# Expert results stored by token and choice; all but the last three blocks read back early, the last three summed by products

## The chip, the cores and the metric

One core of a Trainium2 chip runs the whole kernel. The metric is the device time of one execution in microseconds. TensorE is PE in the profile, its weight loads PEld, VectorE DVE, ScalarE ACT, GpSimd POOL and SyncE SP.

## The reference

Two transformer blocks on 512 tokens of width 1024, all in float32. The first block and the second's mixer are not touched. The change lies in the last layer, a mixture of experts with 32 experts of which each token takes two, and in the last normalisation:

```python
def hierarchical_moe(h, rg_w, rg_b, re_w, re_b, w_gate, w_up, w_down):
    ...
    gate = p_grp * jax.nn.softmax(top_val, axis=-1)
    expert_id = grp[:, None] * EXPERTS_PER_GROUP + top_idx.astype(jnp.int32)
    ...
    def expert_block(args):
        xb, e = args
        a = xb @ w_gate[e]
        u = xb @ w_up[e]
        return (jax.nn.silu(a) * u) @ w_down[e]

    ys = lax.map(expert_block, (xs, block_expert)).reshape(n_slots, D)
    ys = ys * slot_gate[:, None].astype(ys.dtype)
    out = jnp.zeros((T, D), ys.dtype).at[slot_tok].add(ys)
    return out.reshape(B, S, D).astype(h.dtype)

...
        h = rmsnorm(x, norm_ffn_g[l])
        x = x + hierarchical_moe(h, router_group_w[l], router_group_b[l],
                                 router_expert_w[l], router_expert_b[l],
                                 expert_w_gate[l], expert_w_up[l], expert_w_down[l])
    return rmsnorm(x, final_norm_g)
```

`top_val` holds the two best of a token's expert scores, `slot_tok` and `slot_gate` the token and the gate of each place in the padded blocks. w_gate and w_up are 1024x512, w_down is 512x1024: 2 MB each, 6 MB for an expert.

## The kernel before

The program is written by hand, one instruction stream for each engine; semaphores set the order. `Queue.step` lets an instruction raise its engine's semaphore, `run` also waits for it, `wait` waits for other engines' steps.

Dense stages come first (lines 196 to about 1500). At their start GpSimd makes the masks (lines 202 to 214) for which the other engines wait, then index tables (221 to 228). In the first feed-forward stage ScalarE clears the buffer of expert results in HBM, `y_d`, with one transfer of 8 MB (line 427).

Router (1585 to 1720): VectorE finds two experts for each token and a place for each of the 1024 pairs of token and choice. Pairs are cut into blocks of BS = 32 rows of one expert, and the blocks stand in turns of SETS = 3. Products with one-hot tables (1734) give for each block and row the token, a large number where the row is padding. GpSimd gathers a block's rows from `h_d` (1761) by that table. An index beyond the bound is skipped. SyncE loads weights (954), only when the expert of that set of buffers changes; three sets are in use, so the loads for a block are issued when the block three places earlier has finished with the buffer. The loads of the down weights of two sets wait for the first gather (1580).

The block loop (1838 to 2003) runs per block: `gate_up` (1850, the products of 32 rows with both matrices, four groups of 32 columns of the array side by side), transposes of the next block's rows (1768), `down` of the block before (1868), and four products that turn the gated halves (1876). ScalarE copies the first products (1882), applies SiLU (1887), and copies half of the down result (1892); VectorE keeps the turned rows (1809), copies one column of indices (1773), adds the halves of the result into `y_e` (1909) and multiplies (1920). ScalarE then stores `y_e`, 32 rows in two halves of 512 columns, into `y_d` by block position (1902), padding too. GpSimd's part of the loop is the gather for a later block (1950, 1761). The number of turns is computed on the chip.

After the last store GpSimd waits and issues eight indirect loads of 128 rows of 4 KB (2014), one for each tile of 128 tokens and each choice. VectorE multiplies them by the gates and adds them to the tokens (2026), ScalarE squares and sums, VectorE scales by the root (2029 to 2041), and SyncE stores the output (2043).

## Time and profile before

| | us |
|---|---|
| median of 3 runs | 2011.5 (2010.38 to 2014.53) |
| profiled execution | 2010.09 |
| its span | 2008.8 |
| TensorE busy | 1814.8 (90%), granted clock 0.952 |
| VectorE / ScalarE / GpSimd busy | 846.3 / 437.2 / 982.7 |
| HBM read / written | 475.06 MB / 19.66 MB |

The dense stages take the first 1457 us, the router runs to about 1482, the blocks to 1977 and the end of the kernel to 2008.8. Times in all views count from the start of the span. Busy shares are means over stages with different limits, so the stages are read one by one.

### The profile page before, as it was taken

How to read it: one execution, taken by the hardware profiler on the slowest of the kernel's cores; microseconds unless marked ns; L12 is line 12 of the kernel's file. 1: busy time of each engine (PE TensorE's matmuls, PEld its weight loads, DVE VectorE, ACT ScalarE, POOL GpSimd, SP SyncE). 2: the span in 40 equal slices, each digit the busy share in tenths (PEclk: the TensorE clock that was granted, in tenths of full speed). 3: DMA queues.
4: the chain of work that ended last, by engine and by line, in shares of the span. 5: the costliest groups of instructions: out<-in, count | busy, mean ns of one | idle time of the engine just before them, and what ended most of it. 6: DMA issues, size and time to landing. Idle time of an engine off the chain costs nothing.

```text
span 2008.8 us, 27496 instructions
## 1 busy us (share of the span) xinstructions
PE 1814.8 (90%) x9716; PEld 1274.7 (63%) x9716; DVE 846.3 (42%) x1248; ACT 437.2 (22%) x813; POOL 982.7 (49%) x532
## 2 busy tenths in 40 slices
PE   8999999999999899999999889998968978969783
PEld 6888888887676678888888656765733333323231
DVE  6444433310444577444444489876341111111114
ACT  3111100100344432111100144552421111111112
POOL 6888887777444378888887533321211111101001
PEclk9999999999999999999999989999979989979887
DMA  4333372433111133333333212210588999999995
GB/s 160 94 96 102 106 267 88 145 94 94 53 57 50 43 89 91 101 95 94 94 112 100 73 53 73 66 54 28 235 312 325 401 403 399 401 415 412 411 393 207
DMA packets 56977, 346.00 MB, mean 172 GB/s; under 512 B 8474, under 2 KB 8858, under 8 KB 44896
## 3 DMA queue, kind: packets, MB, share of 16 engines
q1 hardware_dynamic: 44640, 315.12, 43.0%
q10 hardware_dynamic: 7968, 19.46, 2.6%
q0 software_dynamic: 4320, 10.78, 1.6%
q8 instruction: 29, 0.48, 0.1%
q14 instruction: 20, 0.16, 0.0%
HBM read 475.06 MB, written 19.66 MB: 246 GB/s over the span
## 4 chain that ended last, share of the span: by engine, by line
PE 71%; DMA 14%; DVE 10%; ACT 3%; issue 1%; POOL 1%; SPq 0%; DVEq 0%; ACTq 0%; POOLq 0%
PE bank L471 31%; PE bank L442 12%; DMA big<-w_up_in 11%; PE bank L1850 7%; PE bank L723 4%; PE bank L1349 4%; PE bank L1868 2%; DVE big L1075 2%; PE bank L490 2%; PE bank L1463 2%; DMA ring<-w_down_in 1%; PE bank L1876 1%; PE bank L641 1%; DVE state L1060 1%; PE bank L701 1%
## 5 line engine op out<-in xcount | busy, mean ns | idle before, releaser
L282 POOL TENSOR_TENSOR weights_hi_parts<-ring,ones 128x1024 fp32r<-128x1024 f32 (+1 forms) x174 | 351.4, 2019 | 291.9 <-PE bank L471 127.7
L284 POOL TENSOR_TENSOR ring_parts<-ring,weights_hi_parts 128x1024 fp32r<-128x1024 f32 (+1 forms) x174 | 468.7, 2693 | 13.6
L471 PE MATMUL bank<-attention_buffers_parts,weights_hi_parts 128*128 128x512 f32 x832 | 325.6, 391 | 11.4 <-DVE ring_parts L510 10.0
L471 PE MATMUL bank<-state_parts,weights_hi_parts 128*128 128x512 f32 x832 | 324.4, 390 | 0.0
L471 PE MATMUL bank<-attention_buffers_parts,ring_parts 128*128 128x512 f32 x832 | 324.2, 390 | 0.0
L1850 PE MATMUL bank<-big,work 128*32 128x512 f32 x1440 | 227.5, 674 | 51.3 <-DMA big<-w_up_in 51.1
L442 PE MATMUL bank<-big_parts,weights_hi_parts 128*128 128x512 f32 x704 | 216.8, 389 | 1.2 <-POOL ring_parts L284 1.2
L1950 POOL TENSOR_TENSOR small<-small 128x1 f32<-128x1 f32 x51 | 9.6, 189 | 375.0 <-DVE small L1773 375.0
L895 POOL TENSOR_TENSOR ring_parts<-ring,weights_hi_parts 128x1024 fp32r<-128x1024 f32 x32 | 80.6, 2520 | 222.6 <-ACT weights_hi_parts L892 222.6
L471 PEld LDWEIGHTS bank<-attention_buffers_parts,weights_hi_parts 128*128 128x128 f32 x832 | 156.6, 188 | 44.8 <-issue 10.5
L471 PEld LDWEIGHTS bank<-state_parts,weights_hi_parts 128*128 128x128 f32 x832 | 156.6, 188 | 33.0 <-issue 0.5
L471 PEld LDWEIGHTS bank<-attention_buffers_parts,ring_parts 128*128 128x128 f32 x832 | 156.6, 188 | 32.8
L442 PEld LDWEIGHTS bank<-big_parts,weights_hi_parts 128*128 128x128 f32 x704 | 132.0, 188 | 29.2 <-POOL ring_parts L284 2.0
L1809 DVE TENSOR_TENSOR work<-bank,cols 128x256 f32<-128x256 f32 x54 | 22.9, 424 | 296.3 <-PE bank L1768 296.3
L1850 PEld LDWEIGHTS bank<-big,work 128*32 128x32 f32 x1440 | 58.1, 122 | 133.0 <-issue 131.5
L442 PE MATMUL bank<-big_parts,ring_parts 128*128 128x512 f32 x352 | 137.0, 389 | 0.0
L413 DVE TENSOR_TENSOR work<-bank,token_scale 128x512 f32<-128x512 f32 x44 | 30.4, 691 | 194.7 <-PE bank L471 194.7
L320 DVE TENSOR_TENSOR big_parts<-work,big_parts 128x512 f32 (+1 forms) x44 | 82.9, 1884 | 42.3 <-ACT big_parts L318 42.3
L1882 ACT ACTIVATE weights_hi<-bank 128x512 f32<-128x512 f32 x54 | 32.3, 597 | 302.7 <-PE bank L1850 302.7
L1850 PE MATMUL bank<-attention_buffers,work 128*32 128x512 f32 x288 | 75.6, 672 | 21.7 <-DMA big<-w_up_in 21.2
L1075 DVE SCALAR_TENSOR_TENSOR big<-big,cols 128x512 f32<-128x512 f32 x105 | 91.5, 919 | 5.9 <-ACT big L1069 5.3
L318 ACT ACTIVATE big_parts<-work 128x512 f32 (+1 forms) x44 | 27.9, 633 | 280.8 <-DVE work L415 280.8
(391 smaller groups left out, 2833.6 us busy)
## 6 DMA issues: line engine op xcount, KB each, us to landing
big<-w_up_in SPq DMA_DIRECT2D x54, 2048.0 KB
ring<-wdense_in SPq DMA_DIRECT2D x176, 512.0 KB, 3.5
state<-w_down_in SPq DMA_DIRECT2D x37, 2048.0 KB
big<-w_gate_in SPq DMA_DIRECT2D x36, 2048.0 KB
attention_buffers<-w_gate_in SPq DMA_DIRECT2D x18, 2048.0 KB
ring<-w_down_in SPq DMA_DIRECT2D x18, 2048.0 KB
ring<-wff_in SPq DMA_DIRECT2D x32, 704.0 KB, 4.1
y_rows<-big ACTq DMA_DIRECT2D x1, 8192.0 KB, 28.0
```

Of the source, the lines that this page charges most:

```text
L282: po.tensor_tensor(hi, raw, ones[:, 0:1].to_broadcast([128, words]), ALU.mult).then_inc(PO.sem, 1)
L284: po.tensor_tensor(lo, raw, hi.bitcast(F32), ALU.subtract) \
L320: return DV.step(dv.tensor_tensor(lo, raw, hi.bitcast(F32), ALU.subtract))
L442: m = pe.matmul(bank, x, y_, start=t + k + n == 0, stop=t == 1 and k == h - 1 and n == 2)
L471: m = pe.matmul(out, x, y_, start=j + n == 0, stop=j == len(pairs) - 1 and n == len(ts) - 1)
L490: m = pe.matmul(banks[t][:, :], x, y_, start=k + n == 0, stop=k == KD - 1 and n == len(ts) - 1)
L723: m = pe.matmul(banks[7][:, :], x, y_, start=k + t == 0, stop=k == KD - 1 and t == 2, skip_group_check=True)
L895: lo_made[n] = PO.step(po.tensor_tensor(lo, raw, hi.bitcast(F32), ALU.subtract))
L1075: last = DV.step(dv.scalar_tensor_tensor(dst, src, w, dst, ALU.mult, ALU.add))
L1349: m = pe.matmul(banks[bank][:, :], x, y_, start=k + j == 0, stop=k == KD - 1 and j == 2, skip_group_check=True)
L1463: m = pe.matmul(bank[:, :], x, y_, start=k == 4 and n == 0, stop=k == 3 and n == 2, skip_group_check=True)
L1850: m = pe.matmul(first_products[b][p:p + BS, :], xet[:, (k + odd) * BS:(k + odd + 1) * BS], sets[b][m_][:, (k + odd) * D_EXP:(k + odd + 1) ...
```

## The change

The buffer of results is now indexed by choice, token and half row: 2048 half rows of 512 numbers and a few spare ones. An indirect DMA by GpSimd scatters each block's 64 half rows (`scatter_step`), in which the indices of padding lie beyond the bound. The half rows of the first partition of each half always have an index within it, if need be that of a spare row. The gates are no longer applied at the end: ScalarE's copy of the first products scales the rows of the up product by their gate (`row_scale`), for which products with the one-hot tables spread the gates over rows (64 more TensorE instructions behind the first `gate_up`). SyncE reads the first choices (`s_pick`) and GpSimd adds the second choices into the tokens by accumulating DMAs (`s_second`) when all turns but the last are scattered. The last three blocks are not stored; one-hot tables made on VectorE (`one_hot`) and products on TensorE (`to_tokens`) sum them by token in PSUM. VectorE adds the first choices (`add_first`) and the banks. The one-hot tables of the router have moved to other buffers; two scale tables became one allocation. GpSimd makes four constant columns at the start with ten more small instructions, VectorE makes three tables of 64x67 in the router (`row_tok`, `row_at`, `added_to`) with four. Tiles 2 and 3 of `to_tokens` follow tile 1 with three calls each. In the diff, cut:

```diff
@@ start @@
-    zeros = big[:, 44 * T:44 * T + D]
+    zeros = big[:, 44 * T:44 * T + 512]
     cleared = PO.run(po.memset(zeros, 0.0))
+    for b in range(SETS):
+        po.dma_start(y_d[4 * T + 2 * b:4 * T + 2 * b + 2, :], zeros[0:2, :]).then_inc(s_y[b], 16)
...
@@ clearing @@
-            ac.dma_start(y_d.rearrange("(n p) c -> p n c", p=128),
-                         zeros.unsqueeze(1).to_broadcast([128, Y_ROWS // 128, D])).then_inc(s_fill, 16)
+            ac.dma_start(y_d[0:4 * T, :].rearrange("(n p) c -> p n c", p=128),
+                         zeros.unsqueeze(1).to_broadcast([128, 4 * NT, 512])).then_inc(s_fill, 16)
@@ router @@
+    DV.step(dv.tensor_scalar(all_but_two.bitcast(I32), turn, -2.0, None, ALU.add))
...
+    def by_rows(bank, cols_, table, copies):
+        for c in range(C2):
+            for g in range(copies):
+                m = pe.matmul(bank[g * BS:(g + 1) * BS, cols_], oh_row[:, c * BS:(c + 1) * BS],
+                              table[:, c * SLOT_COLS:(c + 1) * SLOT_COLS], start=c == 0, stop=c == C2 - 1,
+                              tile_position=(0, g * BS))
+        return m
+    s = PE.step(by_rows(banks[2], slice(0, SLOT_COLS), oh_tok, 2))
...
+    DV.run(dv.tensor_scalar(tokens[:, SETS:], tokens[:, SETS:], NO_ROW + T - 1, None, ALU.bitwise_and))
...
-    DV.run(dv.scalar_tensor_tensor(posf, place, float(BS), rmod, ALU.mult, ALU.add))
-    DV.run(dv.tensor_copy(pos.bitcast(I32), posf))
...
+    gated_slots = DV.run(dv.tensor_tensor(by_slot(oh_gate), by_slot(oh_slot), over_last(gates, C2, SLOT_COLS), ALU.mult))
...
+    dv.wait_ge(s_spread, 1)
+    dv.tensor_scalar(row_scale, banks[7][:, 0:SLOT_COLS], is_up, not_up, ALU.mult, ALU.add).then_inc(DV.sem, 3)
@@ block loop @@
-        ac.activation(gu, first_products[c % SETS][:, :], ACT.Copy).then_inc(AC.sem, 1)
+        ac.activation(gu, first_products[c % SETS][:, :], ACT.Copy,
+                      scale=row_scale[:, bass.ds(i * SETS + c, 1)]).then_inc(AC.sem, 1)
...
-            ac.dma_start(y_d[bass.ds(i * (SETS * BS) + c * BS, BS), half * 512:half * 512 + 512],
-                         y_e[c % SETS][half * BS:(half + 1) * BS, :]).then_inc(s_y[c % SETS], 16)
...
     def dve_result(i, c, steps=1):
+        dv.wait_ge(s_y[c % SETS], i * 16 + (16 * (c // SETS) + 16))
+        dv.tensor_copy(to[c % SETS].bitcast(I32), added_to[:, bass.ds(i * SETS + c, 1)].bitcast(I32)).then_inc(DV.sem, 1)
         dv.wait_ge(AC.sem, at_step(AC, AC_Y, i, c + 1))
-        dv.wait_ge(s_y[c % SETS], i * 32 + (32 * (c // SETS) + 16))
...
+    by_token = y_d[0:4 * T, :].rearrange("(r h) c -> r (h c)", h=2)
+    sp.wait_ge(PE.sem, at_step(PE, PE_GU, laps["sp"], 0))
+    for b in range(SETS):
+        sp.wait_ge(s_y[b], laps["sp"] * 16 + 16)
+    for t in range(NT):
+        sp.dma_start(att[:, t * D:(t + 1) * D], by_token[t * 128:(t + 1) * 128, :]).then_inc(s_pick[t], 16)
...
+    def scatter_step(i, c, n):
+        po.wait_ge(PO.sem, i * (2 * SETS) + (pool_begun + n))
+        po.wait_ge(DV.sem, at_step(DV, DV_Y, i, c + 1))
+        po.tensor_tensor(zo, zc, zc, ALU.add).then_inc(PO.sem, 1)
+        po.indirect_dma_start(y_d[:, :], bass.IndirectOffsetOnAxis(ap=to[c].bitcast(U32), axis=0), y_e[c], None,
+                              bounds_check=4 * T + 1, oob_is_err=False).then_inc(s_y[c], 16)
...
+        for c in range(SETS):
+            gather_step(i, c + 2, 2 * c + 2)
+            scatter_step(i, c, 2 * c + 3)
...
+    for b in range(SETS):
+        po.wait_ge(s_y[b], before_last * 16 + 32)
+    po.wait_ge(s_wexp[2][2], before_last * 16 + 48)
...
+    for t in range(NT):
+        po.dma_start(x_tok[:, t * D:(t + 1) * D], by_token[T + t * 128:T + (t + 1) * 128, :],
+                     accum_op=ALU.add).then_inc(s_second[t], 16)
@@ end, VectorE @@
+    def add_first(t):
+        xt = x_tok[:, t * D:(t + 1) * D]
+        dv.wait_ge(s_pick[t], 16)
+        dv.wait_ge(s_second[t], 16)
+        return DE.run(dv.tensor_tensor(xt, xt, first_rows_at[:, t * D:(t + 1) * D], ALU.add))
...
     dve_mul(laps["dv"], 2)
+    add_first(0)
+    dv.wait_ge(s_y[2], laps["dv"] * 16 + 16)
     dv.wait_ge(AC.sem, at_step(AC, AC_SILU, laps["dv"], 2) + 1)
+    last_sum = DE.step(dv.tensor_tensor(y_e[2], results[2][0:2 * BS, :], y_odd, ALU.add))
+    add_first(1)
@@ end, TensorE @@
+    def to_tokens(t, c):
+        for half in range(2):
+            p = half * BS
+            m = pe.matmul(banks[2 * t + half][:, :], to_token[c][p:p + BS, t * 128:(t + 1) * 128], y_e[c][p:p + BS, :],
+                          start=c == 0, stop=c == SETS - 1, tile_position=(p, 0))
+        return m
+    pe.wait_ge(DV.sem, at_step(DV, DV_Y, laps["pe"], 1))
+    to_tokens(0, 0)
     down(laps["pe"], 2)
+    pe.wait_ge(DV.sem, at_step(DV, DV_Y, laps["pe"], 2))
+    to_tokens(0, 1)
+    to_tokens(1, 0)
+    PE.wait(last_sum)
+    summed = [PT.step(to_tokens(0, 2))]
+    to_tokens(1, 1)
+    summed.append(PT.step(to_tokens(1, 2)))
...
-            for j in range(2):
-                s = DE.run(dv.scalar_tensor_tensor(xt, picked[t][j], gates[:, j * NT + t:j * NT + t + 1], xt, ALU.mult, ALU.add))
+            if t > 1:
+                add_first(t)
+            DE.wait(summed[t])
+            for half in range(2):
+                xh = x_half(t, half)
+                s = DE.step(dv.tensor_tensor(xh, banks[2 * t + half][:, :], xh, ALU.add))
```

## Rows read from the trace of the kernel before

**Rows 1.** Windows: busy us of each engine, granted clock, DMA share, GB/s

```profile
1472.00:1482.00 10.00, 5.61 (x32) 5.23 (x32) 6.61 (x25) 0.00 (x0) 2.17 (x3) 0.50 0.12 42
1486.00:1528.00 42.00, 34.21 (x284) 13.59 (x280) 5.57 (x17) 5.88 (x12) 5.51 (x10) 0.91 1.01 397
1530.00:1560.00 30.00, 30.00 (x275) 12.32 (x278) 6.55 (x18) 6.25 (x14) 4.42 (x8) 1.00 0.76 275
1560.00:1948.00 388.00, 319.32 (x2640) 127.06 (x2636) 57.84 (x164) 60.24 (x123) 45.30 (x82) 0.90 1.01 408
1964.00:1970.00 6.00, 6.00 (x60) 2.66 (x62) 1.35 (x4) 1.39 (x3) 0.00 (x0) 1.00 0.68 265
1970.00:1978.00 8.00, 5.60 (x52) 1.94 (x43) 1.60 (x3) 2.06 (x4) 0.00 (x0) 1.00 0.07 16
```

**Rows 2.** Chain of waits from 1923 us to the end: start, us, what

```profile
1923.66 19.55 DMA big<-w_up_in
...
1972.64 1.05 PE bank L1876 x8
...
1974.44 1.96 PE bank L1868 x16
...
1977.05 0.69 DVE ring L1985
...
1980.44 0.53 issue
1980.97 0.98 POOL big L2014
...
1982.25 5.69 DMA big<-y_rows,small
1987.96 1.29 DVE big L2026
...
1993.24 0.17 DVE small L2029
...
1995.22 1.21 DVE big L2026
...
2004.87 1.28 DVE big L2041
```

**Rows 3.** DMA issues: KB of each, median us from issue to landing

```profile
y_rows<-ring ACTq DMA_DIRECT2D x108, 64.0 KB, 6.8
...
h_rows<-state POOLq DMA_DIRECT2D x4, 512.0 KB, 10.8
out<-big SPq DMA_DIRECT2D x4, 512.0 KB, 2.6
```

**Rows 4.** Queues of the page (packets, MB, share) and its HBM line

```profile
q0 software_dynamic: 4320, 10.78, 1.6%
...
HBM read 475.06 MB, written 19.66 MB: 246 GB/s over the span
```

**Rows 5.** Windows of line 1909 alone, VectorE's sum of a block's result

```profile
1560.00:1943.00 383.00, 27.99 (x41) 0.90 1.01 408
```

**Rows 6.** Timeline of the router's end: start, us, instruction

```profile
1475.80 1.99 PE L471 MATMUL bank<-work 128*32 128x67 f32 x16 [7.47 <-DVE work L1732]
...
1482.31 0.81 SPq L952 DMA_DIRECT2D state<-w_down_in  x2
```

**Rows 7.** Chain of waits in two earlier stretches, 0 to 60 and 1440 to 1700

```profile
22.82 0.86 PE bank L374 x2
...
1497.79 28.12 DMA ring<-w_down_in
```

**Rows 8.** A group of the page: an addition out of PSUM

```profile
L413 DVE TENSOR_TENSOR work<-bank,token_scale 128x512 f32<-128x512 f32 x44 | 30.4, 691 | 194.7 <-PE bank L471 194.7
```

**Rows 9.** Timeline of the program's start

```profile
3.53 0.29 POOL L213 TENSOR_SCALAR_AFFINE_SELECT tri_strict<-ones 128x128 f32<-128x128 f32 x1
...
6.28 1.33 ACT L366 ACTIVATE attention_buffers_parts<-state,cols 128x512 fp32r<-128x512 f32 x2 [3.54 <-DMA cols<-cols_in]
```

More of the change, by code:

```diff
@@ L1663, in build @@
     heads, ids1, key, ahead = sm(3), sm(C2), sm(33), sm(1)
-    pair, total, most, rest, turn = sm(1), sm(1), sm(1), sm(1), sm(1)
+    pair, total, most, rest, all_but_two, turn = sm(1), sm(1), sm(1), sm(1), sm(1), sm(1)
     shift, past, unfilled = sm(2), sm(1), sm(1)
@@ L1700, in build @@
     rank, rdiv, rmod = sm(C2), sm(C2), sm(C2)
-    place, late, posf, pos = sm(C2), sm(C2), sm(C2), sm(C2)
+    place, late, later = sm(C2), sm(C2), sm(C2)
     picks_jn = picks.rearrange("p (j n) -> p j n", j=2)
@@ L1717, in build @@
     DV.step(dv.tensor_scalar(late, place, turn, shift[:, 0:1], ALU.is_ge, ALU.mult))
-    DV.run(dv.tensor_scalar(posf, place, past, shift[:, 1:2], ALU.is_ge, ALU.mult))
-    DV.run(dv.tensor_tensor(late, late, posf, ALU.add))
+    DV.run(dv.tensor_scalar(later, place, past, shift[:, 1:2], ALU.is_ge, ALU.mult))
+    DV.run(dv.tensor_tensor(late, late, later, ALU.add))
     DV.run(dv.tensor_tensor(place, place, late, ALU.add))
-    oh_row, oh_slot = work[:, 512:512 + C2 * BS], work[:, 1536:1536 + C2 * SLOT_COLS]
-    oh_tok, oh_exp = work[:, 2072:2072 + C2 * SLOT_COLS], hi_raw[:, 2 * D:2 * D + C2 * SLOT_COLS]
-    assert 512 + C2 * BS <= 1536 and C2 * SLOT_COLS <= 536 and 2 * D + C2 * SLOT_COLS <= 2 * SLOT
+    n_oh = C2 * SLOT_COLS
+    oh_slot, oh_tok, oh_exp = ring[:, 0:n_oh], ring[:, n_oh:2 * n_oh], hi_raw[:, 2 * D:2 * D + n_oh]
+    oh_gate, oh_row = both_scales[:, 0:n_oh], both_scales[:, n_oh:n_oh + C2 * BS]
+    assert 2 * n_oh <= SETS * 512 and n_oh + C2 * BS <= 2 * T and 2 * D + n_oh <= 2 * SLOT
     def by_slot(x):
@@ L1755, in build @@
     gu, hg, het = hi_raw[:, 2048:2560], hi_raw[:, 2560:2560 + 4 * BS], hi_raw[:, 2688:2688 + 4 * BS]
-    idx = [sm(1) for _ in range(SETS)]
+    idx, to = [sm(1) for _ in range(SETS)], [sm(1)[0:2 * BS, :] for _ in range(SETS)]
     laps = {}
@@ L1778, in build @@
         gather(b, tokens[:, b:b + 1])
-    for q in (PE, AC, PO, DV):
+    PO.wait(counted_laps)
+    laps["po"] = po.value_load(all_but_two[0:1, 0:1].bitcast(I32), min_val=lo - 1, max_val=hi - 1)
+    for q in (PE, AC, DV):
         q.wait(counted_laps)
@@ L1827, in build @@
     AC_GU, AC_Y, AC_SILU = range(1, 4)
-    DV_X, DV_IDX, DV_Y, DV_MUL = range(1, 5)
+    DV_X, DV_IDX, DV_TO, DV_Y, DV_MUL = range(1, 6)
     def at_step(q, k, i, c):
```

117 lines of the change are left out of this document (70 added, 47 removed).

## The prediction

> **What bounds the kernel now.** I read the share of the DMA engines first, then the chain of waits, then the queues, because the diff touches one stage and the end of the program. Up to about 1480 us the kernel is dense matrix work that the diff leaves alone but for a few instructions at the very start. The expert stage behind it is bound by its transfers: from 1560 to 1948 us the 16 DMA engines are busy at a share of 1.01 and move 408 GB/s [rows 1]. TensorE is busy for 319 of these 388 us; the chain of waits shows loads of the up-projection that take 20 us from issue to landing, far longer than 2 MB need at 408 GB/s (5.1 us), since they stand behind other loads [rows 2]. So in this stretch the time is bytes divided by bandwidth. From 1530 to 1560 us the share is 0.76 [rows 1]: there TensorE sets the pace, and bytes saved are worth nothing. From 1943 us on the chain is TensorE again, four more blocks, and then a tail without products: the last sum ends at 1977.74, its rows are stored, GpSimd begins to issue indirect loads at 1980.97, one of them takes 5.69 us to land, VectorE starts at 1987.96 and ends at 2006.15 [rows 2]. These 28.4 us are what the change rebuilds.
>
> **1. Fewer bytes in the saturated stretch.** Before, each of the 54 blocks stores all of its 32 rows of 4 KB in two transfers of 64 KB [rows 3]. The reference has 512 tokens with two experts each, so 1024 of 54 x 32 = 1728 rows are real and 704 (40.7%) are padding. The new store is an indirect one that skips padding. That the chip really moves nothing for a skipped row shows in the software queue: stores of 512 rows of h, 1024 rows read back at the end and 54 gathers of 32 rows of 4 KB would be 13.4 MB if all rows moved; the queue's row has 10.78 MB, which is 1024 real rows in the gathers and few more [rows 4]. In the stretch from 1560 to 1943 us 41 blocks write their results [rows 5]: 41 x 131 KB = 5.37 MB, of which 40.7% = 2.19 MB go away. At 408 GB/s that is 5.4 us. Bounds: 0, if the busiest DMA engine gets no less work, and 7.6 us, if all 54 blocks and a little more counted (54 x 131 KB x 0.407 / 408 = 7.1, and the gathers land sooner). I take -5.4, because the share of 1.01 over the whole stretch leaves no idle time in which the saving could vanish.
>
> The Trainium skill, page "DMA: Bandwidth & Descriptors", section "The descriptor swizzle", speaks against this: it gives each engine four neighbouring partitions. By that rule the filled rows of a block, which lie in its lowest partitions, would keep the same engines as busy as before, and the sum would lose its 5.4 us. No row here names the engine of a packet. It is the second rival below.
>
> **2. What the new store costs its engines.** ScalarE loses two issues per block. GpSimd gains a step per block: a small addition, 0.53 of issue and an indirect DMA of 0.98 us [rows 2], 1.7 us in all. 41 of them add 70 us to the 45.3 that GpSimd is busy in 388 us [rows 1], so it stays two thirds idle. The gather is ahead of the scatter in its queue as on VectorE, so no gather waits behind a scatter whose data come later. VectorE gains one copy of one column; its next sum into the same buffer waits for a scatter from three blocks earlier, and such transfers land in about 7 us [rows 3]. Taken as 0. If the cover were gone, a gather late by 2 us would hold TensorE for as much in each block that TensorE paces.
>
> **3. The front of the stage.** The DMA engines are nearly idle from 1472 to 1482 us (share 0.12 [rows 1]) and the load that ends this starts at 1482.31, behind the first gather [rows 6]. So everything ahead of that gather moves the whole stage. Added there: one VectorE step of some 0.1 us, and a second copy of the products that place the tokens. One copy takes 1.99 us for 16 instructions [rows 6]; the second goes to other columns of the array, as the four groups of L1868 do, where 8 products in 16 instructions take 1.96 us [rows 2] though one alone takes 0.86 [rows 7]. So +0.2, with bounds 0 and +2.1. Behind the gather come five small VectorE operations (0.2 us each), one of 0.7 for the gate table, 64 TensorE instructions for the gates (2 us side by side, 8 one after another) and a wait of the first block's ScalarE copy for them. From 1486 to 1528 us the DMA engines are full (1.01 [rows 1]) and the chain ends in a load of 28.12 us [rows 7], issued into a queue with two earlier pairs of loads in it. These 2 to 8 us lie beside it: 0. Without that cover they would cost 2.5.
>
> **4. The start of the program.** Three small transfers are issued by GpSimd ahead of the masks for which the engines wait. Masks end at 3.82, ScalarE starts at 6.28, when its columns are in [rows 9]. Half the clearing is gone (-0.5), three issues of 0.5 us with gaps of 0.3 and 0.5 ahead of them come in: masks at about 6.1. Cost 0 to 1, taken as +0.2. The table of results that is cleared shrinks by half in a stage with idle DMA: 0.
>
> **5. The tail.** Second choices are added into the token rows by an accumulating DMA from GpSimd and first choices are read by SyncE, four transfers of 512 KB each, when the scatters before the last three blocks have landed; the last three blocks reach the tokens through one-hot products. The one-hot tables (12 small VectorE operations) fall into waits of VectorE. From the rows of the chain and of an addition out of PSUM [rows 2, 7, 8], with 0.86 us for a pair of products (two halves, side by side in different rows of the array):
> TensorE is free at 1973.69; the first pair holds it to 1974.55, so the last down products start 0.11 late and end at 1976.51; copy 0.65 with its gaps, sum 0.69: last sum at 1977.85. Meanwhile two pairs (to 1978.23) and the pair that needs the sum: 1979.1. VectorE adds first choices of tile 1 (1.29) and then two halves out of PSUM at 0.69 each: 1980.6. Tile 1's two pairs end at 1980.8, its halves at 1982.2. Scaling of tile 0 (0.17 + 0.2 + 0.2 + 1.28 with gaps: 1.98): 1984.2. Tiles 2 and 3 cost 1.29 + 1.4 + 1.98 each: 1988.9 and 1993.6; the last scaling ends at 1995.5. Before: 2006.15. That is -10.6.
> The risk is in order: on VectorE the addition of tile 0, which waits for both transfers, stands ahead of the last sum. GpSimd waits for the last down weights, which land near 1969 (the share is 0.68 from 1964 to 1970 us and 0.07 behind it [rows 1]); 0.7 us later it issues. 512 KB land in 2.6 us when stored alone and in 10.8 among other traffic [rows 3]. The trace has no accumulating DMA. Bounded from below by the 512 KB store and from above by that 10.8 for a first tile, it lands between 1973 and 1981, the next ones 1.3 to 9 us apart; it is needed at 1975.7 to cost nothing. Nearest is a shared, otherwise idle queue with twice the traffic (it reads and writes the rows): tile 0 at about 1976.5, a cost of 1.0. I take -9.6 for the tail, bounds -10.6 and -3.
>
> Sum: -5.4 + 0.2 + 0.2 - 9.6 = -14.6. The profiled execution took 2010.09 us (span 2008.8), so 1995.5; the median of the runs shown, 2011.5, lies 1.4 above it. Forecast **1996.9 us**.
>
> **Rivals.** (a) Pairs of products don't run side by side, or TensorE's clock falls from 2.4 to 1.2 GHz in the tail, so that a pair takes 1.72. The same walk gives: last sum 1978.7, tile 0 summed at 1984.0, tile 3's products at 1996.3, end 2001.6; the tail saves 4.5 and the time is 2002.0. For it: the trace shows groups of columns side by side, never of rows. Against: the clock is 1.00 up to 1978 although TensorE has gaps there [rows 1], and the tail now has fewer. The Trainium skill, "TensorEngine Tiling (Array Packing)", section "Tiling Modes", has row tiles work in parallel; that favours the forecast.
> (b) The skipped rows relieve only engines that weren't the last ones, so the stretch keeps its length: 2002.3. For it: a load ends with its slowest engine. Against: the gathers, which have the same skipped rows, leave the share at 1.01 as a mean over all 16.
> (c) Slower than before: the accumulating DMA is slow. All the rest saves about 5 us elsewhere, so the change loses from the point at which the fourth tile lands after 2005 (6.6 us of VectorE's work stand behind it, and 2006.15 + 5 is the mark), that is 2.1 MB in 35 us, 60 GB/s or a seventh of the stretch's rate. At 50 GB/s it lands at 2013 and the end is 2019.6, 13.5 later than now; less the 5 saved elsewhere the time is 2020. For it: no row prices it, and it stands ahead of the last sum. Against: an indirect load of 512 KB on the same queue lands in 5.69 us [rows 2].
> (d) The change doesn't do what it says: readback isn't early, because SyncE and GpSimd wait for the scatters of the last but one lap; if these land 7 us late under load, tile 0 is there at 1981 and the tail saves 5: 2001.5.
>
> **Numbers.** Forecast 0.50; (a) 0.14; (b) 0.18; (d) 0.06; (c) 0.07; two of a, b and d together (about 2007) 0.05. Below: both bounds good, 1991. The range 1991.5 to 2005 leaves out (c), most of the pairs and little below. A measurement of this kernel tells 0.2%, 4 us, from no change. Faster 0.87, same 0.05, slower 0.08.
>
> **What would show it.** Right: written HBM bytes down from 19.7 to about 12.6 MB (4.2 less for the clearing, 2.9 less padding); the last gate and up load landing 5 us earlier; about 19 us from the last sum to the end in place of 28.4; one-hot pairs of 0.9 us. Wrong: a share of 1.0 and the last load at 1943 as before (b); pairs of 1.7 us (a); VectorE waiting for the accumulated rows ahead of the last sum (c, d); a first gather more than 1 us later.

## The result, and the profile after

The changed kernel took 2005.62 us (median of 7 runs, 2004.23 to 2010.76) beside 2012.81 for the kernel before on the same chip (7 runs): ratio 0.9968, 95% interval 0.9956 to 0.998. It is faster by 6.4 us, 4.0 to 8.9; the forecast had 14.6. The profiled execution took 2005.99 us, span 2004.4, against 2010.09 and 2008.8: 4.1 us less. The two numbers differ because the profiled run of before lay under its median.

The queues of the page (packets, MB, share) and its HBM line, after:

```profile
q0 software_dynamic: 6288, 12.81, 2.1%
...
HBM read 475.06 MB, written 15.09 MB: 245 GB/s over the span
```

Three windows of [rows 1] for after, the window of [rows 5] for all engines, and four of the tail: busy us of PE, PEld, DVE, ACT, POOL, granted clock, DMA share, GB/s:

```profile
1486.00:1528.00 42.00, 36.02 (x358) 14.90 (x351) 6.14 (x22) 6.41 (x13) 8.91 (x17) 0.92 1.01 395
1530.00:1560.00 30.00, 30.00 (x276) 12.08 (x272) 6.01 (x20) 6.24 (x12) 9.88 (x17) 1.00 0.81 289
1560.00:1943.00 383.00, 310.65 (x2612) 124.58 (x2608) 61.63 (x205) 63.89 (x123) 91.71 (x164) 0.90 1.00 404
1560.00:1948.00 388.00, 315.65 (x2644) 126.36 (x2638) 61.63 (x205) 64.31 (x124) 91.71 (x164) 0.90 1.00 402
...
1974.00:1976.00 2.00, 2.00 (x12) 0.68 (x8) 0.00 (x0) 1.62 (x2) 0.00 (x0) 1.00 1.07 268
1976.00:1978.00 2.00, 0.21 (x2) 0.00 (x0) 0.00 (x0) 0.46 (x2) 0.00 (x0) 0.81 1.06 223
1978.00:1982.00 4.00, 1.17 (x4) 0.66 (x6) 2.69 (x3) 0.00 (x0) 0.00 (x0) 0.50 1.06 211
1982.00:1986.00 4.00, 4.00 (x12) 1.52 (x10) 1.73 (x3) 1.15 (x2) 0.00 (x0) 0.50 0.78 155
```

The chain of waits that answers to [rows 2]:

```profile
1921.80 20.16 DMA big<-w_up_in
...
1957.28 11.26 DMA state<-w_down_in
...
1969.16 9.49 DMA big<-results_by_token
...
1978.74 1.24 DVE big L2048
...
1980.09 0.69 DVE ring L2066
...
1980.83 15.75 PE bank L2092 x36
...
2000.44 1.28 DVE big L2137
```

DMA issues (KB of each, median us to landing), answering to [rows 3]:

```profile
attention_buffers<-results_by_token SPq DMA_DIRECT2D x4, 512.0 KB, 6.6
big<-results_by_token POOLq DMA_DIRECT2D x4, 512.0 KB, 12.3
results_by_token<-ring,small POOLq DMA_INDIRECT x51, 6.8
```

Timeline lines of the program's start, of the router's end and of the tail:

```profile
6.46 1.33 ACT L381 ACTIVATE attention_buffers_parts<-state,cols 128x512 fp32r<-128x512 f32 x2 [3.74 <-POOL iota_f L230]
...
1476.30 2.00 PE L1757 MATMUL bank<-ring,_squares_and_token_scale 128*32 128x67 f32 x32 [7.51 <-DVE ring L1751]
...
1974.22 1.99 PE L2092 MATMUL bank<-ring,work 32*128 32x512 f32 x8
...
1978.74 1.22 DVE L2048 TENSOR_TENSOR big<-big,attention_buffers 128x1024 f32<-128x1024 f32 x1 [6.73 <-DMA big<-results_by_token]
...
1980.83 2.07 PE L2092 MATMUL bank<-ring,work 32*128 32x512 f32 x4 [4.62 <-DVE ring L2066]
```

Two places hold the difference. The last w_up load lands at 1941.95 instead of 1943.21: the stretch gave 1.3 us, 1.7 counted from the first block's first product (1484.38, before 1483.93). In the window to 1943 us the DMA engines are almost as full as before (share 1.00, before 1.01), but move 404 GB/s instead of 408 [rows 5]. (The 402 of the window to 1948 us has in it 6 us behind the last load, which came 1.3 us earlier than before.) From that landing to the last end it takes 59.8 us instead of 62.9, where the forecast had 53.3. In the chain VectorE waits 6.73 us for accumulated rows, adds them, and only then makes the last sum, which ends at 1980.78. TensorE stands idle for 4.62 us ahead of it; its granted clock falls from 1.00 to 0.81 and 0.50 (2.4 to 1.2 GHz), and its last 36 instructions, 9 pairs of products, take 15.75 us.

### The profile page after: what moved, and what is told of

It reads as the page before. It is cut to its first block, busy times and chain, and to the rows that moved or that the text cites. A ratio compares the mean times of both kernels' runs of the same rounds, so it can differ in the third digit from the quotient of the medians.

```text
span 2004.4 us, 27790 instructions
## 1 busy us (share of the span) xinstructions
PE 1830.3 (91%) x9844; PEld 1282.7 (64%) x9844; DVE 852.8 (43%) x1321; ACT 441.9 (22%) x813; POOL 1043.6 (52%) x643
## 3 DMA queue, kind: packets, MB, share of 16 engines
q0 software_dynamic: 6288, 12.81, 2.1%
HBM read 475.06 MB, written 15.09 MB: 245 GB/s over the span
## 4 chain that ended last, share of the span: by engine, by line
PE 71%; DMA 14%; DVE 10%; ACT 3%; issue 1%; POOL 1%; SPq 0%; DVEq 0%; ACTq 0%; POOLq 0%
PE bank L486 31%; DMA big<-w_up_in 13%; PE bank L457 12%; PE bank L1882 7%; PE bank L740 4%; PE bank L1366 4%; DVE big L1092 2%; PE bank L505 2%; PE bank L1900 2%; PE bank L1480 2%; PE bank L1908 1%; PE bank L658 1%; DVE state L1077 1%; PE bank L718 1%; PE bank L2092 1%
## 5 line engine op out<-in xcount | busy, mean ns | idle before, releaser
L428 DVE TENSOR_TENSOR work<-bank,_squares_and_token_scale 128x512 f32<-128x512 f32 x44 | 30.4, 690 | 194.7 <-PE bank L486 194.7
L1914 ACT ACTIVATE weights_hi<-bank,small 128x512 f32<-128x512 f32 x54 | 37.1, 687 | 309.2 <-PE bank L1882 283.6
L1882 PE MATMUL bank<-attention_buffers,work 128*32 128x512 f32 x288 | 72.1, 645 | 19.0 <-DMA big<-w_up_in 18.4
```

The costliest lines, as they stand in the source:

```text
L1882: m = pe.matmul(first_products[b][p:p + BS, :], xet[:, (k + odd) * BS:(k + odd + 1) * BS], sets[b][m_][:, (k + odd) * D_EXP:(k + odd + 1) ...
```

## The experiments

All are compared with the kernel before on the same chip, and a difference between two of them is that of their ratios times 2012 us. "Length" is the time from the first block's first product to the landing of the last w_up load in the profiled run. It is used because the dense part ahead of it varies: that first product lay anywhere between 1480.8 and 1489.0 us. A length is one profiled run. The changed kernel, e1 and e2 differ only behind the stretch and have 457.6, 457.3 and 456.5; e3, e6 and e8 have 451.9, 452.6 and 453.3. So a difference in length of about 1 us is within what runs differ by, and a difference of two ratios is uncertain by some 3 to 5 us (from their intervals).

| kernel | median us | ratio, 95% interval | length us |
|---|---|---|---|
| before | 2011 to 2013 | 1 | 459.3 |
| changed | 2005.62 | 0.9968, 0.9956 to 0.998 | 457.6 |
| e1_sum_first | 2003.13 | 0.9963, 0.9945 to 0.998 | 457.3 |
| e2_no_accumulate | 2004.36 | 0.9957, 0.9943 to 0.9971 | 456.5 |
| e3_rows_spread | 1999.35 | 0.9948, 0.9932 to 0.9964 | 451.9 |
| e4_padding_stored | 2006.83 | 0.9984, 0.9973 to 0.9994 | 459.3 |
| e5_half_stores | 2004.08 | 0.9963, 0.9952 to 0.9973 | 451.8 |
| e6_plain_reads | 1993.01 | 0.9916, 0.9899 to 0.9933 | 452.6 |
| e7_before_spread | 2006.69 | 0.9976, 0.9965 to 0.9987 | 452.7 |
| e8_reads_behind | 1996.31 | 0.9918, 0.9901 to 0.9934 | 453.3 |
| e9_all_gathered | 2015.87 | 1.002, 1.001 to 1.003 | 467.4 |
| e10_gathered_spread | 2014.59 | 1.0007, 0.9997 to 1.0016 | 467.7 |
| e11_before_gathered | 2021.82 | 1.0034, 1.0022 to 1.0047 | 471.0 |
| e12_upper_rows_skipped | 2006.78 | 0.9976, 0.9966 to 0.9986 | 457.4 |
| e13_odd_rows_skipped | 2001.46 | 0.9943, 0.9929 to 0.9957 | 452.7 |
| e14_spread_all_stored | 2004.25 | 0.9963, 0.9949 to 0.9977 | 454.7 |

### The tail: order, clock, accumulation

e1_sum_first changes the order on VectorE:

```diff
-    add_first(0)
     dv.wait_ge(s_y[2], laps["dv"] * 16 + 16)
     dv.wait_ge(AC.sem, at_step(AC, AC_SILU, laps["dv"], 2) + 1)
     last_sum = DE.step(dv.tensor_tensor(y_e[2], results[2][0:2 * BS, :], y_odd, ALU.add))
+    add_first(0)
     add_first(1)
```

> The changed kernel with the last block's sum ahead of the additions of tile 0's rows on VectorE, nothing else. Theory: the wait for the accumulated rows of tile 0 (landing at 1978.65) held the last sum by 5.1 us and left TensorE idle for 4.6 us, whereupon its clock fell to 1.2 GHz. Now the last sum ends 5 us earlier, the clock stays at 2.4 GHz, a pair of one-hot products takes 0.9 us in place of 1.75, and the end comes 3 to 4 us earlier: ratio to before 0.995. Rival (row tiles run one after another at any clock): pairs take 1.75 us still, end at most 1 us earlier.

Windows of e1, and its chain:

```profile
1974.00:1978.00 4.00, 4.00 (x28) 1.45 (x22) 0.68 (x1) 2.08 (x3) 0.00 (x0) 1.00 1.05 250
1978.00:1982.00 4.00, 4.00 (x22) 1.85 (x20) 1.23 (x1) 0.00 (x0) 0.00 (x0) 1.00 1.06 209
```

```profile
1970.66 11.41 DMA big<-results_by_token
...
1982.20 1.24 DVE big L2048
```

The last sum starts at 1976.10, TensorE doesn't stop, the clock stays at 1.00, and the products run on at 0.88 us a pair (11 pairs, 44 instructions, in 9.71 us). So pairs do run side by side; what made them 1.75 in the changed kernel is the clock, which fell because TensorE stood still. From the last w_up landing to the end it takes 55.3 us, 4.5 less than in the changed kernel. The rest of the gain doesn't come: VectorE now waits for the accumulated rows behind the last sum. Tile 0's let it start at 1979.69, 9.7 us after GpSimd's first issue at 1970.00; tile 1's land 11.41 us after the start given in the chain, and only then do the sums out of PSUM begin:

```profile
1979.69 1.23 DVE L2048 TENSOR_TENSOR big<-big,attention_buffers 128x1024 f32<-128x1024 f32 x1 [2.92 <-DMA big<-results_by_token]
1982.20 1.23 DVE L2048 TENSOR_TENSOR big<-big,attention_buffers 128x1024 f32<-128x1024 f32 x1 [1.28 <-DMA big<-results_by_token]
```

By the ratios e1 and the changed kernel can't be told apart (0.9963 and 0.9968); the gain is in the profile only.

e2_no_accumulate reads the second choices without adding, so that they are left out of the result:

```diff
-        po.dma_start(x_tok[:, t * D:(t + 1) * D], by_token[T + t * 128:T + (t + 1) * 128, :],
-                     accum_op=ALU.add).then_inc(s_second[t], 16)
+        po.dma_start(second_at[:, t * D:(t + 1) * D], by_token[T + t * 128:T + (t + 1) * 128, :]).then_inc(s_second[t], 16)
```

> The changed kernel, with its four late reads of second choices taken without adding, into a free buffer: the second choices of all but the last three blocks are left out of the result. Nothing else moves: GpSimd issues them at the same place, after the last w_down load. Theory (adding in memory makes these transfers move at half rate, and VectorE's first add stands ahead of the last sum): in the profile of the changed kernel the first of them landed 9.49 us after its issue (1978.65), at 211 to 223 GB/s with the DMA engines full; read plainly it should land 4 to 5 us after the issue, about 1974, so that the last sum comes at about 1976 instead of 1980.09, TensorE keeps its clock at 2.4 GHz over the 18 products behind it (about 8 us instead of 15.75), and the time falls by 4 to 8 us, to 1998 to 2002. Rival (the reads are only late because they share the queues with SyncE's reads of the first choices, 2 MB more): landing at 1978 as before, and 2005 to 2006.

A row of its chain, a window, and the last products:

```profile
1969.67 8.40 DMA big<-results_by_token
```

```profile
1974.00:1978.00 4.00, 4.00 (x28) 1.10 (x24) 0.16 (x1) 1.48 (x2) 0.00 (x0) 1.00 0.99 387
```

```profile
1980.26 15.73 PE L2092 MATMUL bank<-ring,work 32*128 32x512 f32 x36 [1.91 <-DVE ring L2066]
```

The chain decides for the rival, for the most part: a plain read lands 8.40 us after its issue, an accumulating one 9.49. The rate does differ: e2 moves 387 GB/s here, where the changed kernel has 268 and 223 in the two halves of this window. But tile 0 has to wait for SyncE's 2 MB beside it in either case. Adding in memory cost 1 to 2 us of the 5 that the sum was late (it ends 37.1 us after the last w_up landing, in the changed kernel 38.8, in e1 33.5); the place of the wait cost the rest. And a shorter wait did not bring the clock back: TensorE is idle for only 1.91 us here, yet the granted clock is at 0.68 from 1978 to 1982 us and at 0.50 behind it, and the 36 instructions take 15.73 us as before. The tail is 58.1 us, 1.7 less than in the changed kernel.

e6_plain_reads takes away both. On top of the spread rows (e3, below), SyncE reads both choices at once; GpSimd adds tiles 2 and 3:

```diff
     for t in range(NT):
         sp.dma_start(att[:, t * D:(t + 1) * D], by_token[t * 128:(t + 1) * 128, :]).then_inc(s_pick[t], 16)
+        sp.dma_start(second_at[:, t * D:(t + 1) * D], by_token[T + t * 128:T + (t + 1) * 128, :]).then_inc(s_second[t], 16)
...
-    po.wait_ge(s_wexp[2][2], before_last * 16 + 48)
...
+    for t in (2, 3):
+        xt = x_tok[:, t * D:(t + 1) * D]
+        po.wait_ge(s_pick[t], 16)
+        PA.run(po.tensor_tensor(xt, xt, att[:, t * D:(t + 1) * D], ALU.add))
+        po.wait_ge(s_second[t], 16)
+        pool_added[t] = PA.run(po.tensor_tensor(xt, xt, second_at[:, t * D:(t + 1) * D], ALU.add))
```

> The changed kernel with the rows of a block spread as in e3_rows_spread (1999.35 us), and in place of the four accumulating reads four plain ones by SyncE, each behind the first-choice read of its tile, without waiting for the last w_down load; GpSimd adds both choices of tiles 2 and 3, VectorE those of tiles 0 and 1. Theory (adding in memory costs twice the engine time, and holds VectorE ahead of the last sum): both choices of tile 0 are there at about 1964 to 1966, the last sum comes at about 1968 instead of 1972.25, the clock stays at 2.4 GHz, and the time is 1989 to 1993. Rival (2 MB more ahead of the last w_down load push that load back by their own 5 us): the last sum comes at 1972 to 1974 as before, the products still run at 2.4 GHz since TensorE waits for a load and not for VectorE in the same way, and the time is 1994 to 1998; 1999 if the clock falls too.

Timeline of its tail:

```profile
1965.24 9.71 PE L2098 MATMUL bank<-ring,work 32*128 32x512 f32 x44
...
1966.00 0.68 DVE L2072 TENSOR_TENSOR ring<-bank,work 64x512 f32<-64x512 f32 x1 [0.58 <-ACT work L2027]
...
1983.80 1.28 DVE L2143 SCALAR_TENSOR_TENSOR big<-big,small,weights_hi 128x1024 f32<-128x1024 f32 x1
```

The last sum waits for ScalarE's copy and for nothing else. It ends 33.2 us after the last w_up landing (38.8 in the changed kernel) and 18.4 us ahead of the end (20.9), at full clock: a tail of 51.6 us against 59.8. Against e3 that is worth 6.4 us. It has the lowest ratio here, 0.84% under the kernel before.

e8_reads_behind puts the second reads behind the last w_down load and the first adds behind the last sum, and moves the three clearing DMAs of the program's start behind the masks:

> e6_plain_reads with three things moved: the four plain reads of second choices wait for the last w_down load, VectorE's first adds stand behind the last sum, and GpSimd's three small clearing DMAs at the program's start stand behind its masks. Theory (a load that TensorE waits for must have nothing beside it; the last sum must not wait for a read): last sum some 2 us after the last w_down product, about 1967, clock 2.4 GHz, both choices of tile 0 at about 1968 to 1970, time 1987 to 1991; ScalarE's first operation at 6.28 again instead of 6.46, and all of the program 0.4 us earlier. Rival (VectorE is what is late: its eight adds of 1.24 us and eight sums of 0.69 us now stand behind one another after the last sum): 1992 to 1996, not under e6_plain_reads.

The rival holds: the sum starts at 1974.84, 33.0 us after the landing (32.6 in e6), but then four adds of VectorE lie behind it, 8.1 us up to the first sum out of PSUM, where e6 has two in 4.5 us, and the tail is 55.5 us. Reading early didn't hold the last sum back. By the ratios e8 and e6 can't be told apart. At the start, ScalarE begins at 6.29 without the three DMAs in front and at 6.23 in e6, which has them. The 0.18 us of the changed kernel's row are within what runs differ by.

### The stretch: bytes, and where they lie

e4_padding_stored gives padding rows spare rows of their own, so that nothing is skipped; e5_half_stores takes half the rows off the direct stores of the kernel before:

```diff
-            ac.dma_start(y_d[bass.ds(i * (SETS * BS) + c * BS, BS), half * 512:half * 512 + 512],
-                         y_e[c % SETS][half * BS:(half + 1) * BS, :]).then_inc(s_y[c % SETS], 16)
+            ac.dma_start(y_d[bass.ds(i * (SETS * BS) + c * BS, BS // 2), half * 512:half * 512 + 512],
+                         y_e[c % SETS][half * BS:half * BS + BS // 2, :]).then_inc(s_y[c % SETS], 16)
```

> The changed kernel, but padding rows are scattered too, each to a spare row of its own, so that every scatter moves all 64 half rows. Theory A (engines of the low partitions set the pace and are as busy either way): the last up-projection load lands within 1 us of the changed kernel's 1941.95, ratio to before about 0.997. Theory B (the skipped bytes save 5.4 us but the scatter costs as much by its packets): the landing is 5 to 6 us later, at about 1947, ratio 0.9995.

> The kernel before, but of each block only the first 16 of 32 rows are stored; the other rows' results are left out. The bytes go down by half on all DMA engines alike: 41 x 65.5 KB = 2.69 MB in the stretch, at 408 GB/s 6.6 us. Theory A (bytes count when every engine is relieved): the last up-projection load lands at 1936 to 1938 in place of 1943.21, ratio 0.9965. Theory C (bytes of stores don't matter in the stretch, since loads and stores go by different paths or another limit holds): landing within 1.5 us of 1943.2, ratio 0.999 to 1.0.

The software queue holds 15.38 MB in e4 and 12.81 in the changed kernel: padding is skipped, 2.57 MB of it. At 408 GB/s that would be 6.3 us. It is worth 1.7 in length and 3.2 in the ratios. ScalarE's queue is 3.53 MB smaller in e5 (19.46 and 15.93), 3.34 MB of it ahead of the last three blocks; that is worth 7.5 and 7.4 us, close to the 8.2 of 3.34 MB. So bytes off the stores can pay nearly in full, and the padding's don't. Full scatters in place of direct stores cost nothing that shows: e4 has the length of the kernel before.

e3_rows_spread deals the ranks of a block over its 32 rows, so that padding no longer lies in the last ones:

```diff
+    row_order = both_scales[:, 2 * T - BS:2 * T]
+    DV.step(dv.tensor_copy(row_order.rearrange("p (s o b) -> p b o s", o=2, b=2),
+                           iota_f[:, 0:BS].rearrange("p (b o s) -> p b o s", b=2, o=2)))
...
-    DV.step(dv.tensor_tensor(by_slot(oh_row), iota_f[:, 0:BS].unsqueeze(1).to_broadcast([128, C2, BS]),
+    DV.step(dv.tensor_tensor(by_slot(oh_row), row_order.unsqueeze(1).to_broadcast([128, C2, BS]),
```

> The changed kernel with one thing different: row j of a block no longer stands in partition j but the rows are dealt out so that any eight neighbouring partitions groups of four get every eighth row (a permuted table of 32 numbers in the router). Theory A (skipped rows relieve only some DMA engines, since filled rows stand together in the low partitions): the filled rows now load all engines alike, so the stretch from 1560 to 1943 us gets shorter; the last up-projection load lands at 1937 to 1939 in place of 1941.95, and the time is 3 to 5 us below the changed kernel's 2005.6, ratio to before about 0.995. Theory B (the scatter costs as much as the skipped bytes save, by its packets): no change, landing at 1941 to 1943, ratio 0.997.

The last w_up load lands at 1933.98, the length falls by 5.6 us and the time by 4.0 against the changed kernel, with the same bytes in every queue. But spreading could ease the gathers as well as the stores. e7_before_spread is the control, the same spreading in the kernel before (with the positions to read back taken from the spread rows):

> The kernel before, with the rows of a block spread over its 32 partitions as in e3_rows_spread and the positions to read back changed to match; every row is still stored. It separates the two things that the spreading may have eased in e3 (8 us at the last w_up load against the changed kernel): the stores, whose skipped rows exist only in the changed kernel, and the gathers of token rows, whose padding is skipped in both kernels. Theory (each DMA engine serves its own partitions, and padding that lies in the last rows leaves the engines of the first rows as they were): the gathers carry 4.49 MB where 51 full ones would be 6.68, so they may give at most 2.19 MB / 408 GB/s = 5.4 us, and at least the 8 - 6.2 = 1.8 us that skipped stores cannot explain: last w_up load 2 to 5 us ahead of 1943.21, time 2006 to 2010, less some 0.5 for two more small VectorE operations at the start of the blocks. Rival (only the stores gained): no change, 2011 to 2012.

It gains 4.8 us (6.6 in length) with no store skipped. So what e3 gained can all have been the gathers', which the change had left as they were. I then tried to take the gathers out of the question by filling them:

```diff
-    DV.run(dv.tensor_scalar(tokens[:, SETS:], tokens[:, SETS:], NO_ROW + T - 1, None, ALU.bitwise_and))
-    DV.run(dv.tensor_scalar(tokens[0:1, SETS:], tokens[0:1, SETS:], T - 1, None, ALU.bitwise_and))
+    DV.run(dv.tensor_scalar(tokens[:, SETS:], tokens[:, SETS:], T - 1, None, ALU.bitwise_and))
```

> The changed kernel, except that padding rows are gathered too (token 0's row in place of a skipped one): up to 6.68 MB gathered where 4.49 MB were, and nothing else. It asks whether bytes taken off the first rows' DMA engines count the same as bytes taken off the others. Theory (rows of a block go to the engines in order, padding lies in the last rows, and the engine that has the first rows ends last; 16 landings of a load lie up to 5 us apart): the 2.19 MB more lie on engines that had time to spare, the last w_up load comes within 1 us of the changed kernel's (457.6 us from the first block's first product), and the time is 2004 to 2007. Rival (what counts is the sum of bytes): 2.19 MB / 408 GB/s = 5.4 us later, 2010 to 2012.

> e9_all_gathered with the rows spread as in e3_rows_spread. All gathers are full here, so that the spreading can only ease the stores, whose padding is skipped. Theory of the engines: the store's share of each engine evens out, so this gains a part of 2.55 MB / 408 GB/s = 6.2 us against e9_all_gathered, at least 3, at most 6, so 1999 to 2003. Rival (the spreading helped the gathers alone; e7_before_spread had 4.8 us of it with no store skipped, and skipped stores save next to nothing in either layout): same as e9_all_gathered within 1 us.

> The kernel before with its padding rows gathered too: every block moves 32 rows in and 32 rows out, the rows in their old order. Theory of the engines: the last engine had every row's share already, no change, 2010.5 to 2013. Rival (bytes): 5.4 us slower, 2016 to 2018.

In e9 and e11 both theories miss. 2.60 MB more in the queue (15.41) cost 9.8 us in length, half as much again as their bytes, and the window of e9 shows a full DMA share at a lower rate than the changed kernel's 403 in the same window (407 before):

```profile
1560.00:1930.00 370.00, 298.23 (x2449) 117.98 (x2442) 57.09 (x190) 59.34 (x114) 85.33 (x152) 0.89 1.01 397
```

e10 and e11 move 397 and 396 GB/s. e10 lies 2.6 us under e9 by the ratios and 0.3 over it in length; e11 is 6.8 us over the kernel before by the ratios, 11.7 in length, in a profiled run that was the slowest of its six. All these added loads read one and the same row, token 0's; that may be what slows them, and no run separates it. So the three say little on where padding lies. (The figure of 5 us between the landings of one load, in the expectation of e9, comes from the trace's landing records, which no view prints; they are read below.)

The clean test leaves the gathers alone. Both kernels are e4 with one more term in the address of the stores, which skips rows 16 to 31 of each half (`m` = 16), or the odd ones (`m` = 1):

```diff
+    DV.run(dv.tensor_scalar(left_out.bitcast(I32), left_out.bitcast(I32), m, None, ALU.bitwise_and))
...
+    DV.run(dv.tensor_scalar(left_out, left_out, 1e6 / m, None, ALU.mult))
...
-                                 last_row[0:2 * BS, b:b + 1], None, ALU.min))
+                                 last_row[0:2 * BS, b:b + 1], left_out[0:2 * BS, :], ALU.min, ALU.add))
```

> e4_padding_stored (the changed kernel with padding stored to rows of its own, 2006.83 us), but the indirect stores skip rows 16 to 31 of each half of a block, whatever they hold: those results are left out. 51 stores of 131 KB lose half, 3.34 MB, as in e5_half_stores, and the gathers stay as they are. Theory of the engines (neighbouring rows go to the same engine, so the engines of the first rows have as much as before): 0 to 2 us less than e4_padding_stored, 2005 to 2007. Rival A (skipped bytes count in full wherever they lie; what was odd in the changed kernel is something else): 3.34 MB / 408 GB/s = 8.2 us less, 1998 to 2000, in e12 and e13 alike. Rival B (a skipped row costs the engines almost what a stored one does): no change in e12 and e13 alike.

> The same kernel with the odd rows of each half skipped in place of rows 16 to 31: the same number of bytes, the same instructions, another place in the block. Theory of the engines: every engine loses half of its share of the store, 6 to 8 us less than e4_padding_stored, 1999 to 2001, and 5 us or more below e12_upper_rows_skipped. Rivals A and B: the same as e12_upper_rows_skipped within 1 us (at 1998 to 2000, or at 2006 to 2007).

Queue and window of e12, then the same of e13:

```profile
q0 software_dynamic: 6288, 12.05, 2.0%
```

```profile
1560.00:1930.00 370.00, 307.07 (x2520) 121.50 (x2519) 59.24 (x199) 61.62 (x119) 88.54 (x158) 0.89 0.99 402
```

```profile
q0 software_dynamic: 6288, 12.05, 2.0%
```

```profile
1560.00:1930.00 370.00, 306.97 (x2575) 122.79 (x2567) 60.15 (x200) 62.47 (x121) 90.34 (x162) 0.91 1.01 406
```

The queue is the same to the last digit, and so are the instructions but for two constants. Against e4 the upper rows are worth 0.0008 of 2012, 1.6 us, which isn't clear of nothing, and the odd rows 0.0041, 8.3 us, about all of the 3.33 MB. The intervals of e12 and e13 don't meet. In lengths it is 1.9 and 6.6. Up to 1930 us e4 moves 407 GB/s. Where neighbouring rows are skipped, the rate falls (402 in e12; 403, 404 and 405 in the changed kernel, e1 and e2); where every second one is, it holds (406). That the place of the skipped rows decides what they are worth is shown. That neighbouring rows share a DMA engine, and that the stretch lasts as long as its busiest engine, is the account that foresaw both numbers; no view names the engine of a packet.

The landing records of the kept traces speak for it. A load of expert weights lands in 16 pieces; the time from its first piece to its last tells how unevenly they were served. Medians over the loads that land between 1560 and 1940 us (55 to 71 a run, those with more than one piece missing from the records left out; the gathers skip padding in all of these kernels):

| kernel | skipped in the scatters | first to last piece, us |
|---|---|---|
| before | no scatters | 2.1 (longest 5.3) |
| e4 | nothing | 3.1 |
| changed | padding, the last rows | 3.6 (e1 3.2, e2 3.8) |
| e12 | rows 16 to 31 | 3.8 |
| e13 | odd rows | 2.7 |
| e14 | nothing, rows spread | 2.2 |
| e3 | padding, rows spread | 2.6 |

The pieces lie furthest apart where neighbouring rows are skipped, and the same bytes skipped at every second row draw them together. Scatters alone spread them a little too (e4 against before), without a cost in time that shows. The finding is one of indirect transfers: e5 leaves out rows 16 to 31 as e12 does, but in direct stores, and there they paid nearly in full.

e14_spread_all_stored is e4 with the rows spread as in e3:

> e4_padding_stored with the rows spread as in e3_rows_spread (1999.35 us, which skips the padding stores). The spreading can ease only the gathers here, since every row is stored. With e3 it prices the skipped stores when the rows are spread. Theory of the engines for the stores: 5 to 6 us above e3_rows_spread, 2004 to 2006. Rival (the spreading eased the gathers alone and skipped padding stores give 1 to 3 us in any layout): 2000.5 to 2002.5, 4 to 6 us below e4_padding_stored, as e7_before_spread lies 4.8 below the kernel before.

With the rows spread, e3 lies 3.0 us under e14 (2.8 in length), for the same 2.57 MB that were worth 3.2 and 1.7 unspread; the spreading itself is worth 4.2 (4.6 in length) where all rows are stored, about as much as in e7. These are the rival's numbers; but the median, 2004.25, lies where the engines' theory had it, and the intervals of e3 and e14 overlap, so 3.0 can't be told from the 5 to 6 of that theory. What is left is that the spreading clearly helps the gathers, and what it adds for the stores isn't settled. The deal is not even either: four neighbouring rows hold the ranks s, s + 8, s + 16 and s + 24, so of a block with 20 real rows four of the eight groups hold three and the others two, and they are the same ones in every such block. If a group shares an engine, the fullest ones shed one row in four, where three in eight are padding. That this is why the stores gain less than their bytes is argued, not shown.

## Why the prediction was wrong

The direction and both places were right, the size was not: in the profiled runs the end came 4.4 us earlier instead of 14.6.

**Step 1, fewer bytes: -5.4, measured -1.7.** The bytes were right: 2.57 MB over 51 stores, where the step's 40.7% of 41 blocks gave 2.19. Their price wasn't (3.2 by the ratios, against 6.3 for the 2.57 MB in full). The step that failed is "the share of 1.01 over the whole stretch leaves no idle time in which the saving could vanish". The share is a mean, and stayed at 1.00; the rate up to 1943 us fell from 408 [rows 5] to 404 GB/s, which over 383 us is 3.8 us, about what is missing between 5.4 and 1.7. The outcome is close to that of rival (b), which had 0.18; its cause, the busiest engines, is what e12, e13 and the landing pieces speak for, though no view names an engine. Its "against", that the gathers with the same skipped rows leave the share at 1.01, was no evidence: spreading those gathers alone gained 4.8 us (e7) at that very share. The rule of the Trainium skill that I set aside, "DMA: Bandwidth & Descriptors", section "The descriptor swizzle", is stated for a transfer to 128 partitions, in which each engine has two groups of four neighbouring partitions, 32 apart. Carried over to these stores from 64 partitions it would have given this outcome; e12 and e13 agree with it.

**Step 2, the new store's engines: 0.** Right. GpSimd is busy for 91.71 us in the stretch, 46 more, not 70: 1.1 a scatter, since the 1.7 that was assumed had 0.53 of issue in it that isn't counted as busy. e4, with all its scatters full, has the length of the kernel before, 459.3.

**Step 3, the front: +0.2.** Right within its bounds. 32 instructions for two copies take 2.00 us where 16 took 1.99 [rows 6], so the second copy is free. The first product came 0.45 later, all of it brought along from ahead of the router (+0.45 at 1455 us already). The gate products lie beside the first loads: the window to 1528 us is full at 1.01.

**Step 4, the start: +0.2.** In the profile +0.18, but e6 and e8 show that it can't be told from 0.

**Step 5, the tail: -9.6, measured -3.2.** Two terms were mis-sized, and they are one cause. The last sum was to end 34.6 us after the last w_up landing, 35.6 with the 1.0 for the wait, and ended 38.8 after it: the wait for tile 0's two reads, priced at 1.0, cost about 5 (without it, in e1, the sum ended 33.5 after the landing). I had seen the order, and named the landing that would cost nothing, 1975.7. The failed step is "tile 0 at about 1976.5", taken in the middle of 1973 to 1981 from rows that had no such read; it came at 1978.65, inside the bounds. From the sum to the end I had 17.7 us and the profile has 20.9, because the clock had fallen in the idle 4.62 us, so that a pair took 1.75 and not 0.86 (15.75 us for 9). I had this as rival (a), with "against" it that the clock stays at 1.00 through gaps up to 1978. In the kernel before the clock had fallen too once the products ended, which the prediction leaves out:

```profile
1976.00:1978.00 2.00, 0.37 (x4) 0.00 (x0) 0.68 (x1) 0.59 (x1) 0.00 (x0) 1.00 0.00 0
1978.00:1982.00 4.00, 0.00 (x0) 0.00 (x0) 0.00 (x0) 1.49 (x2) 1.16 (x2) 0.70 0.13 33
1982.00:1986.00 4.00, 0.00 (x0) 0.00 (x0) 0.00 (x0) 0.00 (x0) 2.84 (x4) 0.50 0.73 213
```

The error was to price the wait and the clock as if they were independent: a late sum makes the idle time, and the clock fell to half in it, in e2 even with 1.91 us of it. The Trainium skill's rule that row tiles work in parallel ("TensorEngine Tiling (Array Packing)", section "Tiling Modes") holds here: the 8 instructions at 1974.22 are 2 pairs in 1.99 us, where four products of 0.86 [rows 7] one after the other would take 3.4.

So what (a) has for the clock and what (b) has for the stretch came together; the other half of (a), pairs one after the other, did not. The text had that pair at "about 2007" with the other pairs at 0.05, and the range ended at 2005. Taken as independent, 0.14 x 0.18 is small; but (a) needed only the wait of rival (c) in a mild form, and that deserved more than it got.

**The signposts.** "Written HBM bytes down to about 12.6 MB" was wrong as a sign: the line says 15.09, and says the same in e4, where all rows are stored. It counts skipped rows; the queue's row doesn't, and is the one to read. Pairs of 0.9 us did show where the clock was up, and VectorE waiting ahead of the last sum was the sign given for a slow accumulation.

## What to carry to other kernels

A DMA share of 1.0 tells that the engines are full on average, not that any byte saved will shorten the stretch: ask which rows stay, and deal them out so that what is skipped is skipped evenly (e13, and e7 for gathers). Keep every wait for a read that is merely convenient behind the one result that TensorE needs, and price an idle TensorE twice: once for the wait, once for the slower products behind it. Shortening the wait pays only the first price: e2 cut the idle time from 4.62 to 1.91 us and its products were as slow. A saving in a tail is only worth what the next thing in its order lets through: e1 freed TensorE and found VectorE waiting for the same reads, and e6, which took the reads early and plain and shared the adds with GpSimd, had the shortest tail.

## What the runs showed of the hardware

- Indirect stores that skip 3.33 MB gained 1.6 us (not clear of nothing) with rows 16 to 31 skipped and 8.3 us with the odd rows skipped, in queues of equal size (12.05 MB). The 16 pieces of a weight load landed 3.8 us apart in the one, 2.7 in the other (medians).
- Filling skipped gather rows with reads of one same row (2.60 MB) cost 9.8 us in length, and the stretch's rate fell from 403 to 397 GB/s at a full share.
- Accumulating reads beside others ran at 268 and 223 GB/s with shares of 1.07 and 1.06 from 1974 to 1978 us, where plain reads made 387 at 0.99; the first 512 KB landed 9.49 us after the issue, against 8.40.
- The granted clock fell from 1.00 to 0.50 over an idle time of 4.62 us and was still 0.50 in the window from 1982 to 1986 us, in which TensorE was busy throughout; the 9 pairs took 15.75 us, 1.75 each, against 0.88 at the full clock. In e2 an idle time of 1.91 us was enough: 0.68 in the window around it, then 0.50, and 15.73 us for the same products.
- The page's HBM line counts the skipped rows of a scatter as written (15.09 MB with and without 2.57 MB skipped); the queue's row does not (12.81 and 15.38 MB).
